# State-space mixer of a streaming encoder: inputs stored in block order, local kernel as two 32-column products over shifted copies

## What is computed

```python
bu = einsum('gpc,bsgc->bsgp', bb, ug)             # complex, with the stream's state added at s = 0
x  = associative_scan(x[s] = ab * x[s-1] + bu[s])
y  = Re(einsum('gcp,bsgp->bsgc', C, x)).reshape(..., 512) + D_skip * u
y  = gelu(y)
y  = y * sigmoid(y @ w_glu + b_glu)
```

## Time and profile before

| | us |
|---|---|
| median of 3 runs | 2441.54 |
| lowest to highest | 2437.79 to 2444.03 |
| profiled execution | 2445.87 |
| its span | 2444.2 |
| PE busy in the span | 2342.9 (96%) |
| POOL, ACT, DVE busy | 447.9, 481.9, 775.2 |

### The profile page before, as it was taken

The page is one execution under the profiler, slowest core; times in us unless marked ns, Lnnn a source line. Parts: engine busy times, 40 slices in busy tenths (PEclk is TensorE's granted clock), DMA queues, the critical chain, the costliest instruction groups (busy, mean ns, idle before and its releaser), DMA issues.

```text
span 2444.2 us, 35648 instructions
## 1 busy us (share of the span) xinstructions
PE 2342.9 (96%) x14349; PEld 2143.4 (88%) x14349; DVE 775.2 (32%) x1245; ACT 481.9 (20%) x798; POOL 447.9 (18%) x260
## 2 busy tenths in 40 slices
PE   6999999999898999999999999999999987999997
PEld 6899999999798999998998988999898885888886
DVE  7221122222121111163644531221231335253533
ACT  6111222122121111111111111111101012243421
POOL 2232222221121222222221221222122120000000
PEclk9999999999999999999999999999999998999999
DMA  5112424141612333332222313332323457455552
GB/s 209 55 58 90 155 73 156 45 171 45 209 56 88 123 120 124 105 106 83 84 84 62 115 59 101 102 105 76 94 99 148 149 170 270 149 213 189 195 202 86
DMA packets 149390, 294.72 MB, mean 121 GB/s; under 512 B 26021, under 2 KB 88721, under 8 KB 145449
## 3 DMA queue, kind: packets, MB, share of 16 engines
q1 hardware_dynamic: 141224, 276.98, 33.4%
q10 hardware_dynamic: 8064, 16.25, 2.0%
HBM read 233.89 MB, written 78.12 MB: 128 GB/s over the span
## 4 chain that ended last, share of the span: by engine, by line
PE 86%; DVE 7%; DMA 5%; SPq 1%; issue 1%; ACT 0%; DVEq 0%; POOLq 0%
PE G L823 19%; PE G L825 18%; PE G L824 18%; PE X L1169 3%; PE X L1171 3%; PE X L1170 3%; PE G L1169 3%; PE G L1171 2%; PE G L1170 2%; PE X L1031 2%; DMA conv_s<-cus 1%; PE X L1010 1%; PE X L1148 1%; PE X L920 1%; PE X L882 1%; PE X L913 1%
## 5 line engine op out<-in xcount | busy, mean ns | idle before, releaser
L823 PE MATMUL G<-hhi,whi 128*128 128x384 f32 x2880 | 991.4, 344 | 7.1 <-POOL wlo L805 2.9
L824 PE MATMUL G<-hlo,whi 128*128 128x384 f32 x2880 | 966.9, 336 | 5.5 <-issue 5.5
L825 PE MATMUL G<-hhi,wlo 128*128 128x384 f32 x2880 | 967.2, 336 | 0.0
L823 PEld LDWEIGHTS G<-hhi,whi 128*128 128x128 f32 x2880 | 543.9, 189 | 34.6 <-issue 18.2
L825 PEld LDWEIGHTS G<-hhi,wlo 128*128 128x128 f32 x2880 | 543.2, 189 | 5.9 <-issue 5.9
L824 PEld LDWEIGHTS G<-hlo,whi 128*128 128x128 f32 x2880 | 544.2, 189 | 1.9
L803 POOL CAST whi<-wr 128x1024 fp32r<-128x1024 f32 x120 | 135.6, 1130 | 1524.2 <-PE G L825 1354.0
L805 POOL TENSOR_TENSOR wlo<-wr,whi 128x1024 fp32r<-128x1024 f32 x120 | 306.6, 2555 | 9.6
L1186 ACT ACTIVATE ev<-G 128x384 f32<-128x384 f32 x180 | 88.0, 490 | 675.1 <-PE G L825 674.9
L1917 DVE TENSOR_TENSOR olo<-orw,ohi 128x1024 fp32r<-128x1024 f32 x96 | 111.8, 1220 | 161.6 <-ACT ohi L1397 161.4
L1169 PE MATMUL G<-ohi,yhi 128*128 128x512 f32 x288 | 114.1, 396 | 23.6 <-DVE ylo L1911 23.6
(11 more groups left out here) (358 smaller groups left out, 2005.5 us busy)
## 6 DMA issues: line engine op xcount, KB each, us to landing
wr<-w_in_t SPq DMA_DIRECT2D x120, 512.0 KB, 5.0
orw<-w_out_t SPq DMA_DIRECT2D x96, 512.0 KB, 5.0
u_scratch<-ev SPq DMA_DIRECT2D x180, 192.0 KB, 1.9
xin<-x_all SPq DMA_DIRECT2D x9, 1024.0 KB, 5.0
cv<-u_scratch SPq DMA_DIRECT2D x16, 576.0 KB, 5.3
yr<-y_scratch SPq DMA_DIRECT2D x12, 768.0 KB, 8.1
xo<-x_all SPq DMA_DIRECT2D x3, 3072.0 KB, 12.4
y_all<-fo SPq DMA_DIRECT2D x9, 1024.0 KB, 4.0
```

The lines of the kernel that those rows point to most:

```text
L823: mm(G[:, j, 0:GC], whi[:, kh, k], hhi[:, kk, hs], start=(kk == 0), stop=False)
L824: mm(G[:, j, 0:GC], whi[:, kh, k], hlo[:, kk, hs], start=False, stop=False)
L825: last = mm(G[:, j, 0:GC], wlo[:, kh, k], hhi[:, kk, hs], start=False, stop=(kk == 15))
```

## The change

The input tiles T = 0..3 are stored in `uT` in block order (step i, then block n): ACT's evacuation permutes (`evac_su`) and SP's store writes pieces of 48 floats. The prompt's blocks come first, and the streams' 16 last. `u4[st]` becomes four tiles of [128, 8, 144], one for each sub-tile (the third shares XS): row group g holds the 32 channels shifted by g steps within the block, with zeros set by DVE in front. The block inputs read them with contiguous columns, but as two products for each weight, 128 prompt columns into banks 0 and 1 and 16 stream columns into bank 4. The local kernel is two weights `Kt[:, hf, st]` (128 rows = 4 taps by 32 channels, 32 columns), applied over the same `u4`; PE writes its taps in this layout, and D is added to the first tap's diagonal by DVE. It opens the sum in banks 2 to 4, right behind the block inputs, and the readout closes it. Gelu reads PSUM and writes T1, which now lies in VT. suP, Kbd, DVE's output step and half of its copies go. DVE makes E5 ahead of AC. The cuts are (0, 6, 9, 18): 6 segments, transposes and taps, 3 segments, block inputs and local kernel, 9 segments, readout. SP loads the next pass's BC and three u4 within the third part, in 14 DMAs. `col` keeps only the 8 columns in use, and the GLU's product is one instruction.

```diff
@@ SP @@
+                if isinstance(T, int) and T <= T_SU(3, 0):
+                    sp.dma_start(uT[T].rearrange("p (i n) -> p i n", i=LC)[:, :, GC // LC * j:GC // LC * (j + 1)],
+                                 ev[:, j].rearrange("p (i n) -> p i n", i=LC)).then_inc(u_stored[j], 16)
...
                 for g in range(4):
-                    src = uT[f, 32 * st:32 * st + 32]
-                    sp.dma_start(u4[st % 2][32 * g:32 * g + 32, 0:NS - 3 + g], src[:, NP + 3 - g:NT]).then_inc(u4_in[st % 2], 16)
-                    sp.dma_start(u4[st % 2][32 * g:32 * g + 32, NS:NT - 3 + g], src[:, 3 - g:NP]).then_inc(u4_in[st % 2], 16)
+                    sp.dma_start(u4[st][32 * g:32 * g + 32, g:LC, :],
+                                 uT[f, 32 * st:32 * st + 32].rearrange("p (i n) -> p i n", i=LC)[:, 0:LC - g, :]).then_inc(u4_in[st], 16)
...
+            def s5(f, last):
                 sp.wait_ge(t1_done, 3 * f + 3)
-                load_u4(f, 0)
+                load_u4(f, 2)
                 gemms(32 + 3 * f, 0, S5_CUTS, 3)
-                sp.wait_ge(su_done, 2 * f + 2)
-                load_u4(f, 1)
                 gemms(32 + 3 * f, 1, S5_CUTS, 3)
                 for n, (t, kh, j) in enumerate(gemm_segs(2, S5_CUTS, 3)):
-                    if n < 2:
-                        sp.wait_ge(x5_mm, 4 * f + n + 1)
-                        load_u4(f, n + 2)
+                    if n == 2 and not last:
+                        sp.wait_ge(ca_done, f + 2)
+                        load_bc(f + 1)
+                        sp.wait_ge(toep_mm, f + 1)
+                        for st in (0, 1, 3):
+                            load_u4(f + 1, st)
                     gemm(32 + 3 * f + t, kh, j)
-                gemms(32 + 3 * f, 3, S5_CUTS, 3)
-                gemms(32 + 3 * f, 4, S5_CUTS, 3)
-                sp.wait_ge(g5_done, 3 * f + 3)
-                sp.dma_start(gS5[f], T1[:, :]).then_inc(g5_stored, 16)
                 sp.wait_ge(xs_done, f + 2)
...
+                if not last:
+                    load_s0(f + 1)
+                sp.wait_ge(t1_done, 3 * f + 6)
+                sp.dma_start(gS5[f], T1).then_inc(g5_stored, 16)
+
+            load_bc(0)
+            load_s0(0)
+            for st in (0, 1, 3):
+                load_u4(0, st)
+            for f in range(4):
+                s5(f, f == 3)
@@ PE @@
                 gemms(32 + 3 * f, 1, S5_CUTS, 3)
                 pe.wait_ge(vt5_ev, 4 * f + 4)
-                pe.wait_ge(su_done, 2 * f + 2)
-                between = list(gemm_segs(2, S5_CUTS, 3))
+                pe.wait_ge(k5_ev, f + 1)
                 for st in range(4):
-                    pe.wait_ge(u4_in[st % 2], 256 * f + 128 * (st // 2) + 128)
+                    pe.wait_ge(u4_in[st], 64 * f + 64)
                     for ri in range(2):
                         for hf in range(2):
-                            last = mm(X[:, st, NC * ri:NC * ri + NC], VT[:, ri, 4 * hf + st], u4[st % 2][:, 4 * hf:NT:LC],
-                                      start=(hf == 0), stop=(hf == 1))
-                    last.then_inc(x5_mm, 1)
-                    if st < 3:
-                        t, kh, j = between[st]
-                        gemm(32 + 3 * f + t, kh, j)
-                gemms(32 + 3 * f, 3, S5_CUTS, 3)
-                pe.wait_ge(k5_ev, f + 1)
+                            for o, n in ((X[:, ri, 128 * st:128 * st + 128], slice(0, NCP)),
+                                         (X[:, 4, XS5 + 64 * ri + 16 * st:XS5 + 64 * ri + 16 * st + NCS], slice(NCP, NC))):
+                                last = mm(o, VT[:, ri, 4 * hf + st], u4[st][:, 3 + 4 * hf, n], start=(hf == 0), stop=(hf == 1))
+                last.then_inc(x5_mm, 1)
+
+                for bk, (i0, i1) in enumerate(Y5_BANKS):
+                    for hf in range(2):
+                        a = max(i0, 4 * hf)
+                        if a < i1:
+                            for st in range(4):
+                                last = mm(X[32 * st:32 * st + 32, 2 + bk, NC * (a - i0):NC * (i1 - i0)], Kt[:, hf, st],
+                                          u4[st][:, a - 4 * hf:i1 - 4 * hf, :].rearrange("p a n -> p (a n)"), start=(hf == 0), stop=False)
+                last.then_inc(toep_mm, 1)
+                gemms(32 + 3 * f, 2, S5_CUTS, 3)
                 pe.wait_ge(ca_done, f + 2)
                 pe.wait_ge(xs_done, f + 2)
...
-                    for t in range(i1 - 1, -1, -1):
-                        a = max(i0, t)
-                        last = mm(X[:, bk, NC * (a - i0):NC * (i1 - i0)], Kbd[:, t],
-                                  suP[:, a - t:i1 - t].rearrange("p a n -> p (a n)"), start=False, stop=(t == 0))
                     last.then_inc(y5_mm, 1)
-                gemms(32 + 3 * f, 4, S5_CUTS, 3)
@@ ACT @@
-                fn(suP[:, :, 0:NCS], T1[:, NP:NT].rearrange("p (n i) -> p i n", i=LC), ACT.Copy).then_inc(su_done, 1)
-                fn(suP[:, :, NCS:NC], T1[:, 0:NP].rearrange("p (n i) -> p i n", i=LC), ACT.Copy).then_inc(su_done, 1)
...
+                for bk, (i0, i1) in enumerate(Y5_BANKS):
+                    act.wait_ge(y5_mm, 3 * f + bk + 1)
+                    fn(T1[:, NC * i0:NC * i1], X[:, 2 + bk, 0:NC * (i1 - i0)], ACT.Gelu_apprx_tanh).then_inc(t1_done, 1)
@@ DVE @@
-            dve.wait_ge(s5_in, 32)
-            v.memset(Kbd[:, :, :], 0.0).then_inc(zero_done, 1)
+            for st in (0, 1, 3):
+                for g in range(1, 4):
+                    last = v.memset(u4[st][32 * g:32 * g + 32, 0:g, :], 0.0)
+            last.then_inc(zero_done, 1)
...
-                dve.wait_ge(bc_in, 48 * f + 48)
-                dve.wait_ge(g5_stored, 32 * f + 16)
+                dve.wait_ge(bc_in, 32 * f + 32)
...
+                c5(v.memset(E5[:, 0, :, 0:1], 1.0))
...
+                dve.wait_ge(t1_done, 3 * f + 3)
+                dve.wait_ge(g5_stored, 32 * f + 16)
+                for g in range(1, 4):
+                    v.memset(u4[2][32 * g:32 * g + 32, 0:g, :], 0.0)
...
                 dve.wait_ge(k5_mm, f + 1)
+                c5(cp(Kt[:, :, :, :].rearrange("p h s c -> p (h s c)"), X[:, 4, 0:256]))
+                dve.wait_ge(s5_in, 32 * f + 48)
+                tt(Kt[0:32, 0].rearrange("p s c -> p (s c)"), X[0:32, 4, 0:128], dD, ADD).then_inc(k5_ev, 1)
```

More of the change, by code:

```diff
@@ L91, in encoder_program @@
         onec = sb(top, "onec", [128, 1])
-        col = sb(top, "col", [128, TT, 96])
+        col = sb(top, "col", [128, TT, 2, 4])
         dec = sb(top, "dec", [128, 4, 16])
@@ L291, in encoder_program @@
         s5_in = sem("s5_in")
-        su_in, bc_in = sem("su_in"), sem("bc_in")
+        bc_in = sem("bc_in")
         s5c = sem("s5c")
@@ L302, in encoder_program @@
         x5_mm = sem("x5_mm")
-        u4_in = [sem("u4_in0"), sem("u4_in1")]
+        u4_in = [sem(f"u4_in{st}") for st in range(4)]
         ca_done = sem("ca_done")
@@ L995, in _ @@
                         last.then_inc(vt5_mm, 1)
-                for t in range(LC):
-                    for st in range(4):
-                        o = X[32 * st:32 * st + 32, 4, 32 * t:32 * t + 32]
+                for st in range(4):
+                    for t in range(LC):
+                        o = X[32 * (t % 4):32 * (t % 4) + 32, 4, 128 * (t // 4) + 32 * st:128 * (t // 4) + 32 * st + 32]
                         mm(o, AC[:, 0, st, t], BC[:, 1, 0, st], start=True, stop=False)
@@ L1218, in _, with evac_su @@
                     root(t + 2)
-            for j in range(3):
-                evac(0, 1, j, ACT.Copy)
+            def evac_su(T):
+                for j in range(3):
+                    act.wait_ge(bank_full, 3 * T + j + 4)
+                    act.wait_ge(u_stored[j], 16 * T + 16)
+                    fn(ev[:, j].rearrange("p (i n) -> p n i", i=LC), G[:, j, 0:GC].rearrange("p (n i) -> p n i", i=LC),
+                       ACT.Copy).then_inc(evac_done, 1)
+            evac_su(0)
             for j in range(3):
@@ L1227, in evac_tile @@
                         evac(T, kh, j, func)
-            evac_tile(1, ACT.Copy)
+            evac_su(1)
             act.wait_ge(gt_dve, GATE_ABS)
@@ L1234, in _ @@
             fn(gB[:, :], gB[:, :], ACT.Ln, bias=1.0).then_inc(gt_act, 1)
-            evac_tile(2, ACT.Copy)
+            evac_su(2)
             act.wait_ge(gt_dve, GATE_ARGS)
@@ L1243, in _ @@
             fn(sm[:, 0], par[:, 2], ACT.Exp).then_inc(s5a, 1)
-            evac_tile(3, ACT.Copy)
+            evac_su(3)
             act.wait_ge(s5v, 1)
@@ L1330, in _ @@
                 evacs(32 + 3 * f, 2, S5_CUTS, [SIGM, SILU, SILU])
-                evacs(32 + 3 * f, 3, S5_CUTS, [SIGM, SILU, SILU])
-                for bk in range(3):
-                    act.wait_ge(t1_done, 3 * f + bk + 4)
-                    fs = slice(432 * bk, min(432 * bk + 432, NT))
-                    fn(T1[:, fs], T1[:, fs], ACT.Gelu_apprx_tanh).then_inc(g5_done, 1)
-                evacs(32 + 3 * f, 4, S5_CUTS, [SIGM, SILU, SILU])
```

(26 more changed lines are left out.)

138 lines of the change are left out of this document (55 added, 83 removed).

## The result

The changed kernel takes 2421.74 us (median of 4 runs, 2421.50 to 2424.59), the kernel before on the same chip 2442.36 (4 runs): a ratio of 0.991, 95% interval 0.9895 to 0.9925, so 20.6 us less. The forecast was 2413 in a range of 2405 to 2422: the measured median lies at its upper end, 0.3 us inside. The profiled execution took 2421.58 us, its span is 2419.8; before they were 2445.87 and 2444.2. So 24.3 us went between the profiled executions, where the sum had 28.4.

A forecast was written before the change was run, and what follows sets the result against it. PE, busy in 96% of the span, was taken as the bound. Four passes at -8.65 us (-34.6), +4.2 for waiting on AC and +2.0 for the clock gave -28.4: median 2441.54 to 2413 us, range 2400 to 2430 (forecast's own 2405 to 2422).

The forecast's parts named there:

- the sum: All terms added: four passes -34.6 us, PE's longer wait for AC +4.2, slower clock behind it +2.0, together -28.4.
- Block inputs: PE's block inputs in each pass: 8.4 us before, 7.3 after for 64 records, so -1.1 us.
- the figure of 25 ns: Skill's time for a matmul of 1 to 64 columns; 16-column records would take 0.8 us a pass, kernel some 12 us shorter.
- (a): Block inputs: 16-column records nearly free, 1.0 us instead of 3.7 per pass, -11 in all, 2402 us; chance 0.07.
- (c): Block inputs: every record costs 0.26 us whatever its columns, 16.6 instead of 7.3 us, +37 in all, 2450; chance 0.05.
- Local kernel: PE's local kernel in each pass: 9.05 us before, 3.1 after with column groups side by side, so -5.95 us.
- the 1.63 us of the earlier trace: PE's idle ahead of the readout, waiting for DVE's scan; to be covered by other work, -1.6 us a pass.
- The start of the stage: First pass: AC 8.4 us later through DVE's new order, +4.2 us of PE waiting, +2.0 for the slower clock.
- Rival (b): Pass ends: clock falls in all three wraps instead of one, +5 us, DVE start at upper bound +3: 2421; chance 0.12.
- the likeliest case: The whole kernel: median goes from 2441.54 to 2413 us, own range 2405 to 2422; chance 0.69.
- "What counts is PE's own work": Bound of the kernel: PE busy in 96% of the span, so its work in the stage and few waits count.
- Rival (d): End of each pass: a formerly hidden load, of u4 or weights, takes back 5 of 8.65 us: 2434; chance 0.07.

## Why the prediction was right or wrong

**The direction and the terms on PE were right.** Block inputs: forecast 7.3 us, measured 7.05, 0.110 for each of 64 records. The value taken from the earlier trace rows for a record of 16 columns, a weight load each, was right; the figure of 25 ns, weighed there from the Trainium skill, was not what such a record costs here, and rivals (a) and (c) fall with it. Local kernel: 3.1 forecast, 3.04 measured, so the column groups do run side by side. No idle stands ahead of the readout: the 1.63 us of the earlier trace rows went. A pass without gaps takes 92.84 us, and the pass of before without its gaps 105.50 - 0.74 - 1.81 = 102.95: 10.1 less, where the sum had 8.65. The sum read readout and local kernel off PE's timeline, where records overlap, as 13.35 us. The chain of waits, by which the new ones are read, has 1.68, 1.61 and 1.12 for the readout and 1.65, 3.83 and 3.84 for the local kernel before, together 13.73; after the change it has 3.04 + 4.06 = 7.10, so 6.6 less. With 1.3 for the block inputs (8.34 to 7.05) and 1.6 for the idle that makes 9.5; the rest, 0.6, was not traced to a row.

**The start of the stage was right in kind and short in size.** AC was ready at about 1067.2 instead of 1059.1, 8.1 us later (forecast 8.4). PE waited 7.78 us, not 6.6, since it came to the wait at 1059.53, 1.4 earlier than the sum had it: the work ahead of the stage ended 1.3 us sooner. Wait and slow clock behind it were forecast as 4.2 + 2.0 = 6.2 over before. What they cost in full is 10.6 us by the run with the tables moved, of which 2.45 were there before, so about 8.

**What was wrong is not in the sum: the wraps of PE's loop.** The working took them as free, though the earlier trace rows had a sign of them: in a pass of 105.50 with PE busy for 101.21 stand 4.3 us of idle, of which the working named 1.63. Another 2.55 are a wrap. Rival (b), "the clock falls at the ends of the passes too", saw the place ("PE's loop now wraps right behind the readout instead of within segments") and half of the effect. The measured median is its 2421, not the 2413 of the likeliest case, but by another make-up: its +5 for the clock, +3 for a late DVE. That the number agrees is luck, and so is in part that the median lies in the forecast's range at all. In the trace the idles grew from 7.8 to 16.3 us, +8.5, which no case had, and the clock fell at three wraps instead of one. For the clock: behind the wait for AC and at the wraps PE worked at 1.2 GHz for 5.7, 4.3, 7.2 and 4.6 us, half of it lost, 10.9 against 3.0 of before (5.9 at the third wrap, from 1355.2 to 1361.1), +7.9.

The sum with what was measured, for the stage from PE's first product to the mLSTM start: passes 4 x -10.1 = -40.4; wait for AC 7.78 - 2.45 = +5.3; idle at the wraps +8.5; clock +7.9; idle ahead of mLSTM 1.38 instead of 3.0, -1.6. That is -20.3; measured are -19.2 (before 1035.6 to 1470.74, after 1034.3 to 1450.17). Ahead of the stage -1.3 and behind it -3.8 make the -24.3 of the profiled executions. These two stretches hold the permuted evacuations, `col` and the GLU's product, which the sum had at nothing; what made them shorter was not traced, and such stretches also differ by some microseconds where nothing in them was changed (the kernel before takes 973.5 us behind the mLSTM start, with the loop written out 968.0).

**Why the change gained less than its work.** With both loops written out it is worth 2436.1 - 2398.0 = 38.1 us, with both as they are 20.6. The missing 17.5 are the wraps: by the medians they cost 23.7 in the changed kernel and 8.3 in the kernel before, 15.4 apart, and the other 2 are what the groups of runs differ by (by the ratios it is 1.0% against 0.3%). Two things make the difference, and the traces of the stage show both: idle and slow clock at the wraps are 24.4 against some 10, and of the 10 the kernel before spends 6.4 on waiting for DVE and SP once they are gone. In the stage that leaves it 3.7; the rest of its 8.3 lies outside of the stage and was not traced. This also corrects the part on what bounded the kernel. "What counts is PE's own work" held for a microsecond or two: at 104.3 to 106.5 us a pass the path over the states' store and load takes over. That the 10.1 us could be kept must be the change's other half, which takes the load of s off that path: this is argued from the code, but in the shifted changed kernel no wait is left in a pass of 92.84. Rival (d) did not occur.

**What stays open.** Why the first gap grew from 0.6 to 3.0 us. A segment behind the readout brings it down to 1.4, so what is queued ahead of the jump matters; but in the kernel before that queue held segments too, and its loop ends at another place of its block, and no run told these two apart. That the loop begins within the last 16 instructions ahead of a block's end, and is brought in again because it then touches eight blocks, fits shifts of 0, 16, 64, 128 and 256 and the shorter body. It is inferred from these; no run shows the addresses. Nor does one show why eight blocks would be too many, since eight are 2048 instructions.

## What to carry to other kernels

Look at the jump back of every loop of the bounding engine before costing a change of its body. Here idle marked "issue", a few instructions, idle again, and packets on the instruction queue at each turn meant that the loop was brought in anew; a shift by a few instructions, a shorter body and a loop written out each cured it. Packets alone don't mean it: written out, the kernel moves 72 of them without a gap. Then check what lies under the bounding engine: writing the loop out was worth 1% in the kernel where PE was the only bound, and 0.3% in the one where a second path was as long. And a wait costs more than its idle when the clock falls behind it (10.6 us for one of 7.8).

## What the runs showed that was not expected

Where code lies changes the kernel's time by 1%: 16 instructions that do nothing, put at the start of the program, take 27 of 80 instruction packets and the gaps at the wraps away, 2411.1 to 2392.0 us (ratios 0.9866 and 0.9777). A shift by 256, ahead of the loop of the changed kernel, leaves packets and gaps as they are.

A satisfied wait is cheap but not free, and two go into one instruction. At the head of the loop PE idles for 4.51, 11.42 and 25.20 us with 64, 128 and 256 such instructions: 6.9 for the second 64, 13.8 for the next 128, so 0.108 each. By this line the first 22 or so cost nothing (an estimate from the three idles), and with 16 PE did not idle; so few instructions are a free way to shift a loop.

At each wrap of the changed kernel stand two idles of 5.3 to 5.6 us together, and TensorE worked at 1.2 GHz for 4.3 to 7.2 us around or behind the second. In the kernel before, with 2.35 to 2.9 us, the clock fell at one wrap of three, and with one segment behind the readout (1.4 and 2.4 us) it still fell at each.
